# Forty-four matmuls whose result nobody reads, in four gaps of a two-model transformer kernel

## The reference

```python
def rms_norm_2(x, g):
    xf = x.astype(jnp.float32)
    y = xf * lax.rsqrt(jnp.mean(xf * xf, axis=-1, keepdims=True) + EPS)
    return (y * g.astype(jnp.float32)).astype(x.dtype)
...
    a_lat = modulate(rms_norm_2(h, norm_mix[i]), sh1, sc1)
    ...
    h = h + g2 * conv_ffn(modulate(rms_norm_2(h, norm_ffn[i]), sh2, sc2), ffn_w_up[i], ffn_conv[i], ffn_w_down[i])
```

## Time and profile before

| | |
|---|---|
| median of 3 executions | 3082.04 us (3081.85 to 3089.59) |
| the profiled execution, its own time | 3081.99 us |
| its span, first to last instruction | 3080.2 us |
| PE busy with matmuls | 2978.4 us, 97% of the span |
| DVE busy | 1819.8 us, 59% |
| ACT busy | 1312.4 us, 43% |
| POOL busy | 520.9 us, 17% |
| granted PE clock, mean | 0.982 |

### The profile page before, as it was taken

How to read it: one execution, slowest core, us unless ns; L and a number is a source line. 1 busy time by engine, 2 the same in 40 slices (tenths; PEclk the granted TensorE clock), 3 DMA queues, 4 the chain that set the end, 5 groups by cost and what they waited for, 6 DMA issues and landing times.

```text
span 3080.2 us, 46647 instructions
## 1 busy us (share of the span) xinstructions
PE 2978.4 (97%) x19342; PEld 2598.9 (84%) x19342; DVE 1819.8 (59%) x2676; ACT 1312.4 (43%) x2276; POOL 520.9 (17%) x464
## 2 busy tenths in 40 slices
PE   6999999999999999999999999998999999999999
PEld 6986666799999999999999987667888878878887
DVE  7676555548768553555867856664544543365353
ACT  4465666433223355663323445553323332243232
POOL 0002323123113100002312323001211201112020
PEclk9999999999999999999999999999999999999999
DMA  3210000025545322003554531102322322223222
GB/s 105 80 52 35 1 2 1 36 102 179 179 159 185 123 94 68 1 35 138 183 181 164 196 123 55 42 1 69 96 96 89 99 86 90 95 76 104 91 91 91
DMA packets 79555, 284.33 MB, mean 92 GB/s; under 512 B 8528, under 2 KB 9296, under 8 KB 78576
## 3 DMA queue, kind: packets, MB, share of 16 engines
q1 hardware_dynamic: 79344, 281.35, 27.5%
HBM read 274.96 MB, written 6.36 MB: 91 GB/s over the span
## 4 chain that ended last, share of the span: by engine, by line
PE 90%; DVE 5%; ACT 3%; issue 1%; POOL 0%; DMA 0%; DVEq 0%; SPq 0%; ACTq 0%; POOLq 0%
PE psum L348 65%; PE psum L2675 2%; PE psum L889 2%; PE psum L1836 2%; PE psum L2047 2%; PE psum L1247 2%; PE psum L2029 1%; PE psum L2020 1%; ACT XH L1360 1%; PE psum L832 1%; PE psum L1270 1%; PE psum L529 1%; PE psum L2372 1%; DVE xt L732 1%; PE psum L2669 1%
## 5 line engine op out<-in xcount | busy, mean ns | idle before, releaser
L303 DVE TENSOR_TENSOR wlo<-wraw,whi 128x1024 fp32r<-128x1024 f32 (+2 forms) x398 | 508.3, 1298 | 629.2 <-ACT whi L296 627.7
L296 ACT CAST whi<-wraw 128x1024 fp32r<-128x1024 f32 (+2 forms) x398 | 396.4, 1022 | 514.4 <-PE psum L348 482.7
L431 DVE CUSTOM_DVE_ANT_0 araw<-araw,cond 128x1024 f32<-128x1024 f32 x112 | 181.1, 1655 | 0.0
L348 PE MATMUL psum<-f0xh,whi 128*128 128x264 f32 x704 | 143.7, 286 | 4.9 <-DVE f0xl L574 3.3
L348 PE MATMUL psum<-f1xh,whi 128*128 128x258 f32 x704 | 142.5, 284 | 4.8 <-DVE f1xl L574 3.3
L348 PE MATMUL psum<-f2xh,whi 128*128 128x512 f32 x352 | 140.3, 399 | 3.5 <-DVE f2xl L570 3.5
L348 PE MATMUL psum<-f3xh,whi 128*128 128x512 f32 x352 | 140.3, 398 | 3.5 <-DVE f3xl L570 3.5
L348 PE MATMUL psum<-f0xh,wlo 128*128 128x264 f32 x704 | 143.5, 285 | 0.0
L348 PE MATMUL psum<-f0xl,whi 128*128 128x264 f32 x704 | 143.1, 285 | 0.0
L348 PE MATMUL psum<-f1xh,wlo 128*128 128x258 f32 x704 | 142.5, 284 | 0.0
L348 PE MATMUL psum<-f1xl,whi 128*128 128x258 f32 x704 | 142.0, 283 | 0.0
(11 more groups left out here) (532 smaller groups left out, 8414.4 us busy)
## 6 DMA issues: line engine op xcount, KB each, us to landing
wraw<-d_w SPq DMA_DIRECT2D x357, 512.0 KB, 3.4
araw<-d_ada SPq DMA_DIRECT2D x112, 512.0 KB, 3.3
wraw<-d_w SPq DMA_DIRECT2D x32, 384.0 KB, 3.4
hn<-d_h SPq DMA_DIRECT2D x4, 528.0 KB, 7.4
hres<-d_h SPq DMA_DIRECT2D x1, 2112.0 KB, 8.2
spill<-hres SPq DMA_DIRECT2D x1, 2112.0 KB, 7.4
hres<-spill SPq DMA_DIRECT2D x1, 2112.0 KB, 8.5
cond<-d_cond SPq DMA_DIRECT2D x2, 1024.0 KB, 4.9
```

Source lines behind the costliest of these rows:

```text
L296: e.copy(whi[0:rows, n % NH, 0:kt * cols], wraw[0:rows, n % NR, 0:kt * cols]).then_inc(*w_hi.up(n))
L303: e.tensor_tensor(wlo[0:rows, n % NH, 0:kt * cols], wraw[0:rows, n % NR, 0:kt * cols], whi[0:rows, n % NH, 0:kt * cols].bitcast(F32), ALU. ...
L348: ins = e.matmul(psum[0:bw, b0 + nb * len(sl) + si, 0:ln], l_ if z == 2 else h_, (xp.lo if z == 1 else xp.hi)[:, k, o:o + ln], start=k == ...
L431: e.tensor_tensor_reduce(out=w, in0=w, in1=self.c[:, col, :], scale=1.0, scalar=0.0, op0=ALU.mult, op1=ALU.add, accum_out=ada[:, ly, blk, ...
```

## The change

A helper `keep_warm` is added. It waits until the first chunk of the projection behind the norm is rounded, and issues eleven matmuls with the chunk's first 128 columns as stationary operand and its first 512 columns as moving operand into a PSUM bank that is not in use. Nothing reads the result; the projection's own first matmul into the bank starts it afresh. It is called right behind the sums in `ffn_pe` for f2 and f3 (bank 4), in `sbp_pe` (bank 2) and in `sc_pe` (bank 6). The norms of f0 and f1 are left as they are.

```diff
+        def keep_warm(e, tag, bank):
+            n = chunks_of(tag, 0)[0][0]
+            e.wait_ge(*w_hi.at(n))
+            for _ in range(11):
+                e.matmul(psum[:, bank, 0:512], whi[:, n % NH, 0:128], whi[:, n % NH, 0:512], start=True, stop=True)
...
             start(e)
             rms_pe(e, f, ntok, F.sq, 0)
+            if f in ("f2", "f3"):
+                keep_warm(e, (f, "up", 0), 4)
             for half in range(2):
...
             rms_pe(e, "sb", L, sqs, 0)
+            keep_warm(e, "sbq", 2)
...
             rms_pe(e, "sc", LX, sqx, 0)
+            keep_warm(e, "scin", 6)
```

## The result

The changed kernel took 3077.75 us (median of 20 executions, 3072.6 to 3084.54) against 3084.26 us for the kernel before (20 executions, 3079.27 to 3091.66). The ratio is 0.9977, with a 95% interval from 0.9969 to 0.9984: 7.1 us less, between 4.9 and 9.6. It is faster, but the 7.1 us are less than the 9.2 us (0.3%) that were set as the mark and less than the 10.5 us forecast, and the time lies 1.75 us above the range. The kernel before, too, was 2.2 us slower over 20 executions than over the three whose median the sum started from.

The account below looks back on a forecast made before the run. The prediction took TensorE (PE) to bound the kernel, slowed by half clock behind four gaps. Added work cost 0 and the held clock gave 10.5 us: 3082.0 − 10.5 = 3071.5 us, range 3066.5 to 3076 with the second case.

Parts of the forecast that it names:

- What bounds the kernel: TensorE (PE), 90% of the chain; unbroken matmuls behind the four gaps, with 5.58 to 6.17 us at half clock in each.
- The waits and the eleven matmuls cost nothing: In the four gaps: waits on `w_hi` are already met; eleven matmuls of 0.2335 us, 2.57 us in all, cost 0.
- The room was larger than stated: Eleven matmuls fit f2's 3.49 us gap with 0.92 us to spare, and sbq's 3.31 us with 0.74 us.
- the added matmuls did not run at the pace of the sums: Rival: at 0.86 us each the added matmuls delay the first products, 24.2 us for the four, so 3095.7 us; chance 0.05.
- the clock did not fall all the same: Rival: the clock still falls behind the four filled gaps, nothing won or lost, 3082 us; chance 0.09.
- VectorE keeps ahead, and the third chunk is in time: Behind the four gaps: VectorE needs 1.32 us per k, PE 1.40 (sbq 1.47); third chunk's slack 0.95 us; loss 0.0 to 0.4 each.
- the prediction's 1.5 us of slow products: Behind f0's norm: 3.41 us of products at half clock cost 1.5 us.
- whose gap it let rise by 1.3 us: Inside a rival: once sbq saves 2.5 us, f1's gap moves and its cost may rise from 1.5 to 2.8 us.
- What the clock gives back: Products behind f2, sc, f3 and sbq run at full instead of half clock: 2.65, 2.80, 2.53 and 2.51 us, 10.5 in all.
- The base: Time of the kernel before that the sum started from: 3082.0 us, after the shown runs' median of 3082.04.
- part is given back elsewhere: Rival: other gaps move and grow dearer, 1.5 to 4 us lost, 6.5 to 9 us remain, 3073.0 to 3075.5; chance 0.28.
- the 10.24 us stretch may go: Inside a rival: the half-clock stretch at 1230.82, around the first attention scores, may shrink by 3.4 us or more.

Follow-up runs that it names:

- e4: Twenty-two instead of eleven matmuls in each of the changed kernel's four gaps; 0.9988 of the kernel before.
- e2: The changed kernel with eleven matmuls behind the sums of all six norms, f0 and f1 too; 0.9967 of the kernel before.
- e1: The kernel before, unchanged, profiled a second time; ratio 0.9995.
- e11: The changed kernel, unchanged, a fourth profile; 2398.4 us from f0's last sum to the end.
- e14: The kernel before with the eleven matmuls in the gaps of f2, sc and f3 only, not sbq's; ratio 0.9990.
- e12: The changed kernel with all six norms' gaps filled, and sixteen matmuls in the gap ahead of wino; 0.9967 of the kernel before.
- e16: Second profile of the kernel before with only the gaps of f2, sc and f3 filled; 2398.1 us from f0's last sum to the end.
- e3: Five instead of eleven matmuls in each of the changed kernel's four gaps; 0.9982 of the kernel before.
- e8: The changed kernel's eleven matmuls with 128 columns in place of 512; half clock behind sbq, f2, sc, f3: 0, 3.0, 3.4, 0 us.
- e7: Three instead of eleven matmuls in each of the changed kernel's four gaps; half clock behind sbq, f2, sc, f3: 0, 3.0, 3.4, 0 us.

## Why the prediction was wrong in size and right in kind

**What bounds the kernel: right.** The chain's pieces behind the four places shortened by 2.56, 2.64, 2.80 and 2.54 us, and the stages with them.

**The waits and the eleven matmuls cost nothing: right.** The first product has the same releaser. The pitch is that of L348: twenty-two in 5.35 us in e4, with the last one's 0.39 us taken off 0.236 us each. The room was larger than stated (1.27 us, not 0.92), since the stated one used modelled ends. Two rivals are excluded: the added matmuls did not run at the pace of the sums, and the clock did not fall all the same, in sixteen gaps of sixteen.

**VectorE keeps ahead, and the third chunk is in time: right** for the four places. For f0 the prediction's 1.5 us of slow products is a price that the kernel doesn't pay: by e2 the time goes into waits instead when the clock holds. The same is true of f1, whose gap it let rise by 1.3 us: f1's part of the kernel took 378.2 us in all 18 profiles.

**The step that failed: "What the clock gives back", the sum 2.65 + 2.80 + 2.53 + 2.51 = 10.5 us.** Each term is right for that execution and wrong as the size of the effect. It took the stretches of one profile as what the kernel pays in every execution. Over six profiles with the gap open, sbq paid 5.66, 5.99, 0, 5.63, 5.98 and 0 us at half clock, and the three last gaps together cost 947.7, 942.6, 947.7, 947.8, 945.4 and 947.8 us of stages against 939.7 us filled: 6.8 us on average and not 8.0. With the 1.9 us for sbq that is 8.7 us, and four profiles against four give 8.5. The prediction had this in hand: it saw in the earlier trace rows that equal gaps pay differently, and applied it to the gaps behind the change, not to the four themselves. The profile it read was the dearest of the cases, drawn twice in four. Of the 6.2 us by which 3077.75 missed 3071.5, 2.0 are this term.

**The base.** 3082.04 us was the median of three; 20, 28, 12 and 21 executions gave 3084.26, 3084.25, 3085.28 and 3085.07. This moved the time by another 2.2 us. With the right base and 8.5 us of gain, 3075.8 us would have been inside the range; the last 2.0 us lie between the 8.5 us of the profiles and the 6.5 us between the two medians, inside the noise of both. The scatter is mostly the clock's: over the 20 executions of the changed kernel the time falls by 2.2 us for each 0.001 of mean granted clock, from 3081.8 us on average at 0.981 to 3073.4 at 0.985; over the 28, 12 and 21 of the kernel before it falls by 1.5, 1.7 and 1.8 us. (The 1.4 us of e1's expectation rests on a slip: 0.001 of the mean clock is 6.2 us at half clock, not 3.1, since half clock takes half away, and at 0.4535 us each they cost 2.8 us where PE sets the time throughout.)

**The rival "part is given back elsewhere"** got the size (6.5 to 9 us) for a reason that isn't shown, so that this was luck. The stage from f1 to f2 is 2.0 us longer in four profiles against four, the one from sbq to f1 is 1.8 us shorter beyond sbq's own gap. Both differences are within their scatter, and they cancel. Right in kind was that the 10.24 us stretch may go (e11); the +1.3 us for f1 was wrong.

**Open.** Profiles and timings don't quite agree on the last three gaps. By the stages they are worth 6.8 us; e14 timed 3.1 us, 5.9 at most. If all executions that aren't profiled drew e1's cheap case (942.6 us), they would be worth 2.9 us, which is about what was timed; but no unprofiled execution shows its stages. Their mean clock leans the same way. In the six profiles with these gaps open 6.8 to 20.5 us at half clock began in them or just behind, 17.1 on average, which is 0.0028 of the mean clock. e14's eleven executions have 0.9813 on average, the 21 of the kernel before beside them 0.9801: only 0.0012 more, with a standard error of 0.0006. So the executions timed either lost less clock there than those profiled, or lost more elsewhere. Whether sbq's saving shifts the later ones toward other prices stays open as well.

## What to carry to other kernels

A half-clock stretch behind a gap is a draw, not a constant. Before a sum is made from it, take several profiles of the same kernel, cut them into stages, and use the mean; the profiled stretch says what kind of effect there is. Fill a gap only where PE is the late one behind it (look at what hands it the next operand, and whether it would keep ahead at twice the pace), and size the filling by the starts of instructions, so that about 1 us is left, as here, and nothing is pushed.

## What the runs showed of the hardware that was not expected

- The same gap of 3.5 us (f3) was followed by 5.6 us of products at half clock in three profiles of the kernel before and by none in another (e1). A fall is not the certain price of such a gap.
- Half clock behind a gap costs nothing where PE isn't the late one: f1's part took 378.2 us with 0, 3.4 and 6.8 us of it (e2, the kernel before, e11).
- Ahead of a projection's first product, with 0.7 to 1.0 us of idling left, no fall was seen in 36 cases (sixteen of the changed kernel, twenty of e2 and e12 to e16); after 2.1 to 2.3 us there were three in eight (e3, e8); after 2.6 to 2.8 us two in four (e7). Elsewhere the length of the last wait is no such guide: behind the 1.19 us at 1227.02 the clock did fall.
- Eleven matmuls of 128 by 128 with a weight load each step 0.126 us at full clock, no faster than those of 264 columns (0.122 us): half the width brought no shorter step.
